# Retention chunks rotated by GpSimd during attention, their low parts split in two halves on VectorE

## The chip, the cores and the metric

The kernel runs on one core of a Trainium2 chip. The metric is the device time of one execution in microseconds (us). The engines are TensorE (PE; PEld is its weight load), VectorE (DVE), ScalarE (ACT), GpSimd (POOL) and SyncE (SP), which issues most transfers.

## What is computed

One decoder layer over 1024 tokens of width 1024: a projection of the normed input, a branch of causal attention (8 heads), a branch of chunkwise retention (4 heads), both gated, merged, projected out, added to the input and normed. The change concerns the retention branch, which in the reference reads:

```python
q = rotary(q.reshape(B, S, H, RET_QK), positions)
k = rotary(k.reshape(B, S, H, RET_QK), positions) * (RET_QK ** -0.5)
def step(R, chunk):
    qc, kc, vc = chunk
    inner = jnp.einsum('bhqk,bhkd->bhqd', jnp.einsum('bhqd,bhkd->bhqk', qc, kc) * decay_in[None], vc)
    cross = jnp.einsum('bhqd,bhde->bhqe', qc, R) * xi[None, :, :, None]
    R = R * gamma_c[None, :, None, None] + jnp.einsum('bhkd,bhke->bhde', kc * zeta[None, :, :, None], vc)
    return R, inner + cross
mu = jnp.mean(out, axis=-1, keepdims=True)
var = jnp.mean(jnp.square(out - mu), axis=-1, keepdims=True)
out = ((out - mu) * lax.rsqrt(var + EPS)).reshape(B, S, RET_WIDTH) * g_ret
```

## The kernel before

Every float32 product is made of three matmuls on rounded operands (fp32r): high times high, high times low, low times high. ScalarE makes the high part of a tile (a Copy), VectorE the low part (tile minus high part), so each operand costs both an instruction. All engines run a program written out by hand and meet at semaphores; each is strictly in order, and so is SyncE's list of transfers.

**Attention** (about 750 to 1080 us) has 64 steps g: head h = g // 8, block of 128 queries i = g % 8. TensorE makes the scores of step g, matmuls of filler work (the retention values v, in units of 24 matmuls that go through `v_stage` to memory), every second step the product with the values of a head, and the transposes of the probabilities of step g - 1. VectorE takes the row maximum (L2021), ScalarE the exponential (L1551), VectorE scales by the reciprocal (L2042, `prob`), and both split the transposed probabilities (L1564, L2052). Every second step VectorE multiplies a pair of outputs by the head's gate (L2033, `y_full`); the gates of two heads are held in two buffers `head_gate`, loaded by `load_head_gate` (L921). ScalarE's queue loads the values of a head, `v_head` (L914). SyncE loads q and k of a head (L904 to L908) and stores `y_full` (L940).

**Retention** (about 1080 to 1340 us) has 32 steps n: head n // 8, chunk n % 8. TensorE: `outputs(n)`, `state(n)` (not in the last chunk of a head), filler (rest of the v work in the first steps, then the merge product of the attention branch, L2504), `turn_keys(n + 1)`, `inner_scores(n + 1)`, filler, `turn_outputs(n)` (L2660), filler. VectorE in step n (`vector_retention`, L2124): a few merge units, bn_stats of the outputs (L2137), bn_aggr (L2140), then it waits for ScalarE's square root (L1620), reciprocal (L2142) and two small instructions, the low part of the state (L2153), `low_chunk(n + 1)`, the gated output `y_ret` (L2163), the low part of q and k of chunk n + 2 (`low_qk`, L1598), and in some steps the low part of a merge weight (L616) or of an attention output tile (`y_lo`, L2183). ScalarE makes the root, the high part of the state, the normed output `out_n` (L1630), which `turn_outputs` waits for, and the high parts (`high_qk`, L1594).

The rotation of q and k is GpSimd's: `rotate_chunk` (L1262) runs four instructions per chunk on a raw chunk of 128x512 and its cosine and sine (L1277, L1279, L1281, L1282), in place, in one of three buffers `qk_raw`. Chunks 0 and 1 are rotated at the end of attention, the other 30 within retention. GpSimd also makes the token sums of each pair of outputs (`token_sums`, L1224: four instructions of 128x256, L1231 to L1238). SyncE's `load_qk_chunk` loads raw chunk and tables three or four steps ahead.

Of the kernel before, what the change touches and what calls it, by code (L numbers as in the profile page):

```python
# [14 lines left out]
F32 = mybir.dt.float32  # L15
F32R = mybir.dt.float32r
# [96 lines left out]
PAIR_CHUNKS = NT // 2  # L113
GROUPS_SPLIT = ((0, 1), (2,), (3,), ())
# [34 lines left out]
class Layer:  # L149
# [3 lines left out]
    def __init__(self, nc, sem, a, t, d, out, pools):  # L153
# [66 lines left out]
        self.head_gate = z("head_gate", 40, [P, 2, S])  # L220
# [5 lines left out]
        self.qk_raw = [z("qk_raw_%d" % n, kb, [P, 6, P]) for n, kb in enumerate((56, 59, 4))]  # L226
        self.qk = z("qk_chunk", 62, [P, 2, 8, P], F32R)
        self.by_sine = [z("qk_by_sine_early", 98, [P, 4, P]), z("qk_by_sine", 0, [P, 4, P])]
        self.v_chunk = [z("v_chunk_%d" % n, kb, [P, 2, RET_V], F32R) for n, kb in enumerate((52, 40, 48))]
# [83 lines left out]
    def semaphores(self, sem):  # L313
# [14 lines left out]
        self.x_late = sem("x_t_late_ready")  # L328
# [31 lines left out]
        self.roped = sem("k_pe_roped")  # L360
# [36 lines left out]
        self.gc_loaded = [sem("gate_chunk_loaded_%d" % n) for n in range(3)]  # L397
        self.qk_step = sem("qk_rotation_step")
# [19 lines left out]
        self.t_sums_done = sem("token_sums_done")  # L418
# [20 lines left out]
        self.out_hi_ready = sem("out_w_hi_ready")  # L439
# [343 lines left out]
    def sync(self, sp):  # L783
# [93 lines left out]
        self.load_head_gate(sp, 1)  # L877
# [40 lines left out]
    def load_head_gate(self, sp, h):  # L918
        if h >= 2:
            sp.wait_ge(self.y_done, 4 * (h - 1))  # L920
        sp.dma_start(self.head_gate[:, h % 2, :], self.d["act_t"][h]).then_inc(self.head_gate_loaded[h % 2], 16)  # L921

    def sync_attention(self, sp):
        d = self.d
        parts = 0
        for g in range(STEPS + 4):
# [3 lines left out]
            if i == 5 and 1 <= h < H_MLA - 1:  # L930
                self.load_head_gate(sp, h + 1)
# [4 lines left out]
            if g >= 4 and g % 2 == 0:  # L936
# [4 lines left out]
                    .then_inc(self.y_stored[pair % 2], 16)  # L941
            if g == STEPS - 6:
# [16 lines left out]
            if g == STEPS + 2:  # L959
                self.load_qk_chunk(sp, 2)  # L960
                self.load_qk_chunk(sp, 3)
                self.load_set0(sp, 1)

    def load_qk_chunk(self, sp, n):
        if n >= 3:
            sp.wait_ge(self.k_turned, n - 2)
            sp.wait_ge(self.qk_lo_ready, n - 2)
        h, m = divmod(n, NT)
        sp.dma_start(self.qk_raw[n % 3][:, 0:4, :].rearrange("p c n -> p (c n)"), self.d["qk"][h, m])\
            .then_inc(self.chunk_loaded[n % 3], 16)  # L970
# [1941 lines left out]
```

## Time and profile before

| | us |
|---|---|
| Median of 3 runs | 1586.63 (1585.99 to 1589.74) |
| Profiled execution, its own time | 1586.35 |
| Its span in the profile | 1584.5 |
| TensorE busy | 1540.6 (97%) |
| VectorE busy | 994.8 (63%) |
| ScalarE busy | 667.4 (42%) |
| GpSimd busy | 415.9 (26%) |

The span is what the profile shows of the execution, 1.85 us less than its time. A busy TensorE is one with a matmul under way; a 128x512 matmul is shown with about 0.39 us though the next one starts 0.23 us after it, so gaps shorter than 0.16 us do not show as idle. Time that is lost shows as idle time or as a granted clock (PEclk) below 1. The shares are means over stages with different limits, so the stages are read apart.

### The profile page before, as it was taken

The page shows a single profiled execution, that of the slowest core. Times are in us where ns is not written, and L with a number is a line of the kernel's source. Part 1 is how long each engine was busy: PE and PEld are TensorE (multiplying, and loading weights), DVE is VectorE, ACT ScalarE, POOL GpSimd, SP SyncE. Part 2 cuts the span into 40 slices and gives each one's busy share as a digit, 9 for nine tenths or more (in the row PEclk, how much of TensorE's full clock was granted, in tenths as well). Part 3 has the DMA queues.
Part 4 walks back from the last instruction along what each step waited for, and adds up shares of the span by engine and source line. Part 5 has one row for each costly group of instructions (what it writes and reads, how often), then busy time and mean ns, then how long its engine had stood idle before and what let it go on. Part 6 is the DMA issues. An engine that isn't in the chain of part 4 may idle for free. (4 is left out here: it accounts for less than half of the span.)

```text
span 1584.5 us, 20414 instructions
## 1 busy us (share of the span) xinstructions
PE 1540.6 (97%) x7472; PEld 1287.2 (81%) x7472; DVE 994.8 (63%) x1629; ACT 667.4 (42%) x1144; POOL 415.9 (26%) x350
## 2 busy tenths in 40 slices
PE   5999999999999999999999999999899999999998
PEld 4788888888888888788888888887677888878886
DVE  6884444444444458752666665667988877799644
ACT  7553455543333353342343343434544444445311
POOL 0032233222322200200000000017778783522000
PEclk9999999999999999999999999999999999999999
DMA  9333232333323334699365554546988787889432
GB/s 381 104 136 113 107 113 107 114 108 118 120 106 107 94 108 156 260 413 339 134 207 176 173 200 172 186 140 229 307 268 265 255 271 240 297 286 309 156 107 80
DMA packets 154499, 299.55 MB, mean 189 GB/s; under 512 B 12048, under 2 KB 93072, under 8 KB 145696
## 3 DMA queue, kind: packets, MB, share of 16 engines
q1 hardware_dynamic: 137680, 265.80, 48.5%
q10 hardware_dynamic: 12080, 15.60, 2.9%
q0 software_dynamic: 4640, 16.84, 2.7%
q8 instruction: 60, 0.98, 0.3%
q14 instruction: 39, 0.32, 0.1%
HBM read 196.23 MB, written 100.93 MB: 188 GB/s over the span
## 5 line engine op out<-in xcount | busy, mean ns | idle before, releaser
L1894 DVE TENSOR_TENSOR w_form<-w_pair,w_form 128x512 fp32r<-128x512 f32 x150 | 116.3, 776 | 124.9 <-ACT w_form L1469 123.2
L1469 ACT ACTIVATE w_form<-w_pair 128x512 fp32r<-128x512 f32 x150 | 94.7, 632 | 216.8 <-PE p_banks L2433 211.7
L1551 ACT ACTIVATE prob<-p_banks,neg_max 128x128 f32<-128x128 f32 (+3 forms) x64 | 47.4, 741 | 183.1 <-DVE neg_max L2021 183.1
L1286 POOL DMA_DIRECT2D v_ret<-v_stage x32 | 17.5, 548 | 399.8 <-DVE v_stage L1998 399.5
L2430 PE MATMUL p_banks<-h_hi,w_form 128*128 128x512 f32 x300 | 116.7, 389 | 0.0
L2432 PE MATMUL p_banks<-h_lo,w_form 128*128 128x512 f32 x300 | 116.7, 389 | 0.0
L2433 PE MATMUL p_banks<-h_hi,w_form 128*128 128x512 f32 x300 | 116.7, 389 | 0.0
L1196 POOL TENSOR_TENSOR w_pair<-w_pair 128x512 f32<-128x512 f32 x25 | 32.5, 1299 | 235.4 <-DVE w_form L1894 235.4
L2712 PE MATMUL p_banks<-t_hi,w_hi 128*128 128x512 f32 x224 | 87.5, 390 | 2.2 <-DVE t_lo L1662 2.2
L2715 PE MATMUL p_banks<-t_hi,w_lo 128*128 128x512 f32 x224 | 87.2, 389 | 0.0
L2714 PE MATMUL p_banks<-t_lo,w_hi 128*128 128x512 f32 x224 | 87.2, 389 | 0.0
L616 DVE TENSOR_TENSOR w_lo<-w_raw,w_hi 128x1024 fp32r<-128x1024 f32 (+3 forms) x63 | 66.8, 1063 | 27.7 <-ACT w_hi L595 27.0
L2472 PE MATMUL p_banks<-w_hi,h_hi 128*128 128x512 f32 x192 | 78.5, 409 | 0.6 <-DVE w_lo L616 0.6
L2430 PE MATMUL p_banks<-h_sum_hi,w_form 128*128 128x512 f32 x200 | 77.8, 389 | 0.0
L2432 PE MATMUL p_banks<-h_sum_lo,w_form 128*128 128x512 f32 x200 | 77.8, 389 | 0.0
L2433 PE MATMUL p_banks<-h_sum_hi,w_form 128*128 128x512 f32 x200 | 77.8, 389 | 0.0
L2430 PE MATMUL p_banks<-h_forms,w_form 128*128 128x512 f32 x200 | 77.8, 389 | 0.0
L2432 PE MATMUL p_banks<-h_forms,w_form 128*128 128x512 f32 x200 | 77.8, 389 | 0.0
L2433 PE MATMUL p_banks<-h_forms,w_form 128*128 128x512 f32 x200 | 77.8, 389 | 0.0
L595 ACT ACTIVATE w_hi<-w_raw 128x1024 fp32r<-128x1024 f32 (+3 forms) x63 | 53.1, 847 | 57.8 <-PE p_banks L2347 13.0
L2472 PE MATMUL p_banks<-w_lo,h_hi 128*128 128x512 f32 x192 | 76.4, 398 | 0.0
L2472 PE MATMUL p_banks<-w_hi,h_lo 128*128 128x512 f32 x192 | 76.2, 397 | 0.0
(348 smaller groups left out, 4482.7 us busy)
## 6 DMA issues: line engine op xcount, KB each, us to landing
w_pair<-in_w_pairs SPq DMA_DIRECT2D x25, 1024.0 KB, 4.8
v_ret<-v_stage POOLq DMA_DIRECT2D x32, 512.0 KB, 3.7
v_chunk<-v_ret SPq DMA_DIRECT2D x32, 512.0 KB, 3.9
w_raw<-in_w_ret SPq DMA_DIRECT2D x28, 512.0 KB, 5.5
w_raw<-in_w_dense SPq DMA_DIRECT2D x23, 512.0 KB, 5.8
act_t<-stage SPq DMA_DIRECT2D x40, 256.0 KB, 2.0
act_t<-stage_late SPq DMA_DIRECT2D x40, 256.0 KB, 2.0
ada<-in_w_ada SPq DMA_DIRECT2D x4, 2048.0 KB, 24.9
```

The costliest lines, as they stand in the source:

```text
L595: self.nc.scalar.activation(self.hi_place(r), self.split_source(r), ACT.Copy).then_inc(self.w_hi_ready, 1)
L616: self.nc.vector.tensor_tensor(self.lo_place(r), self.split_source(r), self.hi_place(r).bitcast(F32), ALU.subtract)\
L1469: self.nc.scalar.activation(self.form[f % FORM_SLOTS][:, 0, :], self.form_source(f), ACT.Copy).then_inc(self.form_hi, 1)
L1551: nc.scalar.activation(self.prob[:, g % 2, 0:width], p[:, 6:8, :].rearrange("p a n -> p (a n)")[:, 0:width], ACT.Exp, bias=self.neg_max[:, ...
L1894: nc.vector.tensor_tensor(self.form[f % FORM_SLOTS][:, 1, :], self.form_source(f), self.form[f % FORM_SLOTS][:, 0, :].bitcast(F32), ALU.su ...
L2430: self.nc.tensor.matmul(out, w_hi[:, cut], x_hi[:, q, :], start=fresh and q == 0, stop=False, skip_group_check=True)
L2432: self.nc.tensor.matmul(out, w_hi[:, cut], x_lo[:, q, :], start=False, stop=False, skip_group_check=True)
L2433: last = self.nc.tensor.matmul(out, w_lo[:, cut], x_hi[:, q, :], start=False, stop=q == KD // 2 - 1, skip_group_check=True)
L2472: ins = self.nc.tensor.matmul(self.p[:, FILL_BANKS[unit % 3], :], h[:, k, tok], w[:, cut], start=(k == 0 and kind == 0), stop=(k == KD - 1 ...
L2712: self.nc.tensor.matmul(out, self.w_hi[:, slot, cut], x_hi, start=fresh and k == 0, stop=False, skip_group_check=True)
L2714: self.nc.tensor.matmul(out, self.w_hi[:, slot, cut], x_lo, start=False, stop=False, skip_group_check=True)
L2715: done = self.nc.tensor.matmul(out, self.w_lo[:, slot, cut], x_hi, start=False, stop=k == KD - 1, skip_group_check=True)
```

## The change

The rotation moves out of retention. In attention, every second step, SyncE (`move_rotation`) stores the chunk that was rotated before to `d["qk"]` and loads the next one with its tables into a place of its own (`rot_raw`, `rot_table`); GpSimd rotates it into `by_sine`. In retention the loaded chunk is the rotated one, with no tables (128 KB fewer per chunk), and TensorE and ScalarE wait for its load instead of GpSimd. To make room, `head_gate` has one buffer instead of two: the gate of head h + 1 is loaded when the last `y_full` of head h is done. `v_chunk` 1 and 2 change places, and their first loads move. `low_qk` becomes two instructions of 128x256: the second half of chunk n + 1 stands behind bn_aggr of step n, ahead of the reciprocal; the first half of chunk n + 2 where the whole was. Some semaphores are shared, with counts that go on from an earlier use. The diff, without the semaphores' names:

```diff
@@ load_head_gate (one buffer)
-        if h >= 2:
-            sp.wait_ge(self.y_done, 4 * (h - 1))
-        sp.dma_start(self.head_gate[:, h % 2, :], self.d["act_t"][h]).then_inc(self.head_gate_loaded[h % 2], 16)
+        if h:
+            sp.wait_ge(self.y_done, 4 * h)
+        sp.dma_start(self.head_gate[:, :], self.d["act_t"][h]).then_inc(self.head_gate_loaded[h % 2], 16)
@@ sync_attention
-            if i == 5 and 1 <= h < H_MLA - 1:
-                self.load_head_gate(sp, h + 1)
...
+                if q == NT // 2 - 1 and head < H_MLA - 1:
+                    self.load_head_gate(sp, head + 1)
+            if g >= 2 and g % 2 == 0:
+                self.move_rotation(sp, g // 2 - 1)
...
-            if g == STEPS - 1:
-                sp.wait_ge(self.y_done, 4 * (H_MLA - 1))
-                self.load_v_chunk(sp, 1)
             if g == STEPS + 1:
                 sp.wait_ge(self.score_done, STEPS)
-                self.load_v_chunk(sp, 2)
+                self.load_v_chunk(sp, 1)
...
+                sp.wait_ge(self.y_done, 4 * H_MLA)
+                self.load_v_chunk(sp, 2)
                 self.load_set0(sp, 1)
+
+    def move_rotation(self, sp, n):
+        if n:
+            h, m = divmod(n - 1, NT)
+            sp.wait_ge(self.qk_step, 4 * n)
+            sp.dma_start(self.d["qk"][h, m], self.by_sine[:, :, :].rearrange("p c n -> p (c n)")).then_inc(self.rot_stored, 16)
+        if n < CHUNK_STEPS:
...
+            sp.dma_start(self.rot_raw[:, :, :].rearrange("p c n -> p (c n)"), self.d["qk"][h, m]).then_inc(self.rot_loaded, 16)
+            sp.dma_start(self.rot_table[:, :, :], self.d["ret_tables"].rearrange("a p n -> p a n")[:, :, m * P:(m + 1) * P])\
+                .then_inc(self.rot_loaded, 16)
@@ gpsimd
-            if g == STEPS - 2:
-                for n in range(2):
-                    self.rotate_chunk(pool, n)
-        for n in range(2, CHUNK_STEPS):
-            if n == 9:
+            if g % 2 and 1 <= g // 2 <= CHUNK_STEPS:
+                self.rotate_chunk(pool, g // 2 - 1)
+        for k in range(1, CHUNK_STEPS, 2):
+            self.token_sums(pool, k)
+            if k == 3:
                 for unit in range(units, FILL_UNITS):
                     self.store_fill(pool, unit)
-            self.rotate_chunk(pool, n)
-            if n >= 4 and n % 2 == 0:
-                self.token_sums(pool, n - 3)
-        for k in (CHUNK_STEPS - 3, CHUNK_STEPS - 1):
-            self.token_sums(pool, k)
@@ low_qk
-    def low_qk(self, dve, n):
+    def low_qk(self, dve, n, half):
         dve.wait_ge(self.qk_hi_ready, n + 1)
-        self.nc.vector.tensor_tensor(self.qk[:, n % 2, 4:8, :], self.qk_raw[n % 3][:, 0:4, :],
-                                     self.qk[:, n % 2, 0:4, :].bitcast(F32), ALU.subtract).then_inc(self.qk_lo_ready, 1)
+        blocks = slice(2 * half, 2 * half + 2)
+        self.nc.vector.tensor_tensor(self.qk[:, n % 2, 4 + 2 * half:6 + 2 * half, :], self.qk_raw[n % 3][:, blocks, :],
+                                     self.qk[:, n % 2, blocks, :].bitcast(F32), ALU.subtract).then_inc(self.qk_lo_ready, 1)
@@ vector_retention
             nc.vector.bn_aggr(self.mean_var[:, s, :], self.stats[:, s, :]).then_inc(self.stats_done, 1)
+            if n + 1 < CHUNK_STEPS:
+                self.low_qk(dve, n + 1, 1)
             dve.wait_ge(self.rooted, 6 + n + 1)
...
             if n + 2 < CHUNK_STEPS:
-                self.low_qk(dve, n + 2)
+                self.low_qk(dve, n + 2, 0)
```

On VectorE, in a retention step behind the outputs' statistics, there stood (`mean_var` is what bn_aggr makes, `ret_rstd` the reciprocal root):

```order
L2140 BN_AGGR mean_var<-stats 128x2
L2142 RECIPROCAL ret_rstd<-ret_root 128x1
L2145 TENSOR_SCALAR ret_rstd<-ret_rstd,ret_cols 128x1
L2148 TENSOR_SCALAR ret_shift<-mean_var,ret_rstd 128x1
L2153 TENSOR_TENSOR state_lo<-p_banks,state_hi 128x512 x2
```

and now:

```order
L2150 BN_AGGR mean_var<-stats 128x2
L1605 TENSOR_TENSOR qk_chunk<-qk_raw_122,qk_chunk 128x256
L2154 RECIPROCAL ret_rstd<-ret_root 128x1
L2157 TENSOR_SCALAR ret_rstd<-ret_rstd,ret_cols 128x1
L2160 TENSOR_SCALAR ret_shift<-mean_var,ret_rstd 128x1
```

A half of a chunk's low parts now stands ahead of the reciprocal. At the end of step 4 of retention there stood on VectorE:

```order
L2121 TENSOR_TENSOR inner_lo<-p_banks,inner_hi 128x128
L2163 TENSOR_TENSOR y_ret_stage_135<-p_banks,gate_chunk 128x512
L1598 TENSOR_TENSOR qk_chunk<-qk_raw_120,qk_chunk 128x512
L2183 TENSOR_TENSOR y_lo_168<-y_raw_169,y_hi_167 128x1024
L2183 TENSOR_TENSOR y_lo_171<-y_raw_172,y_hi_170 128x1024
```

and now:

```order
L2131 TENSOR_TENSOR inner_lo<-p_banks,inner_hi 128x128
L2175 TENSOR_TENSOR y_ret_stage_136<-p_banks,gate_chunk 128x512
L1605 TENSOR_TENSOR qk_chunk<-qk_raw_120,qk_chunk 128x256
L2195 TENSOR_TENSOR y_lo_169<-y_raw_170,y_hi_168 128x1024
L2195 TENSOR_TENSOR y_lo_172<-y_raw_173,y_hi_171 128x1024
```

Here 128x512 became 128x256; the rest is as it was. On SyncE, where one attention head hands over to the next (`q_odd`, `k_odd` are the operands of the head after it), there stood:

```order
L940 DMA y_mla<-y_full 128x256 x2
L904 DMA q_odd<-q_hl 128x2048
L905 DMA k_odd<-k_hl 128x2048
L908 DMA q_rope_odd<-qr_hl 32x1024 x4
L940 DMA y_mla<-y_full 128x256
L921 DMA head_gate<-act_t 128x1024
```

and now:

```order
L940 DMA y_mla<-y_full 128x256
L923 DMA head_gate<-act_t 128x1024
L971 DMA qk_chunks<-qk_by_sine 128x512
L979 DMA rotation_raw<-qk_chunks 128x512
L980 DMA rotation_table<-ret_tables 128x2x128
L906 DMA q_odd<-q_hl 128x2048
L907 DMA k_odd<-k_hl 128x2048
L910 DMA q_rope_odd<-qr_hl 32x1024 x4
```

The gate's load moved ahead of q and k, from one `y_full` later, and the store and two loads of a rotation stand between them.

## Rows read from the trace of the kernel before

**Rows 1.** Stretches of the program: busy time of each engine, clock, DMA.
```profile
core 0: us, PE busy (x) PEld busy (x) DVE busy (x) ACT busy (x) POOL busy (x), PEclk, DMA share, GB/s
760.00:1080.00 320.00, 319.79 (x1851) 278.20 (x1850) 205.06 (x436) 120.37 (x262) 23.88 (x36) 1.00 0.49 169
1084.30:1119.20 34.90, 32.45 (x153) 26.20 (x152) 29.34 (x67) 18.14 (x35) 26.73 (x26) 0.95 0.79 264
1119.20:1156.20 37.00, 30.02 (x137) 22.35 (x137) 34.15 (x69) 18.03 (x33) 29.19 (x27) 0.95 0.93 319
1156.20:1216.00 59.80, 57.70 (x293) 47.49 (x291) 49.31 (x127) 27.21 (x57) 48.21 (x48) 1.00 0.80 255
1216.00:1314.00 98.00, 97.80 (x494) 81.37 (x493) 79.50 (x205) 44.31 (x93) 78.58 (x79) 1.00 0.80 257
```

**Rows 2.** Who TensorE waited for, 1084 to 1330 us (total, times, longest).
```profile
PE p_banks L2660 <- ACT out_n L1630: 8.8, 8, 2.5
```

**Rows 3.** Timeline of all engines, end of retention step 4 and start of 5.
```profile
1125.09 4.54 DVE L2183 TENSOR_TENSOR y_lo<-y_raw,y_hi 128x1024 fp32r<-128x1024 f32 x2
...
1126.40 2.15 POOL L1279 TENSOR_TENSOR qk_raw<-qk_raw 128x512 f32<-128x512 f32 x1
...
1129.56 0.68 DVE L2137 BATCH_NORM_STATS2 stats<-p_banks 128x6 f32<-128x512 f32 x1
...
1131.74 0.78 ACT L1630 ACTIVATE out_n<-p_banks,ret_shift,ret_rstd 128x512 f32<-128x512 f32 x1
...
1132.57 0.66 PE L2660 MATMUL p_banks<-ident,out_n 128*128 128x128 f32 x4 [2.49 <-ACT out_n L1630]
```

**Rows 4.** VectorE's groups by form, 1119.4 to 1156.1 us.
```profile
L2183 DVE TENSOR_TENSOR y_lo<-y_raw,y_hi 128x1024 fp32r<-128x1024 f32 x5 | 9.7, 1966 | 0.0
...
L1598 DVE TENSOR_TENSOR qk_chunk<-qk_raw,qk_chunk 128x512 fp32r<-128x512 f32 x4 | 3.6, 904 | 0.0
L616 DVE TENSOR_TENSOR w_lo<-w_raw,w_hi 128x1024 fp32r<-128x1024 f32 x2 | 3.5, 1754 | 0.0
...
L2118 DVE TENSOR_TENSOR k_tok<-p_banks,k_tok 128x256 fp32r<-128x256 f32 x4 | 1.7, 417 | 0.4 <-ACT k_tok L1606 0.4
```

**Rows 5.** VectorE's groups by form in attention, 760 to 1060 us.
```profile
L616 DVE TENSOR_TENSOR w_lo<-v_weight_raw_odd,w_hi 128x1024 fp32r<-128x1024 f32 x6 | 7.3, 1224 | 0.6 <-ACT w_hi L595 0.3
...
L2042 DVE TENSOR_SCALAR prob<-prob,recip 128x1024 f32<-128x1024 f32 x7 | 5.3, 754 | 0.2
```

**Rows 6.** GpSimd's groups by form, 1084 to 1314 us.
```profile
L1279 POOL TENSOR_TENSOR qk_raw<-qk_raw 128x512 f32<-128x512 f32 x30 | 41.6, 1386 | 2.4
...
L1237 POOL TENSOR_TENSOR y_ret_stage<-y_ret_stage,y_ret_stage 128x256 f32<-128x256 f32 x14 | 11.2, 800 | 1.1
```

**Rows 7.** Who VectorE waited for, 1084 to 1330 us.
```profile
DVE ret_rstd L2142 <- ACT ret_root L1620: 14.1, 31, 0.5
```

**Rows 8.** Timeline in attention where one head hands over to the next.
```profile
838.31 0.53 ACTq L914 DMA_DIRECT2D v_head<-v_hl  x1
...
841.38 0.41 DVE L2033 TENSOR_TENSOR y_full<-p_banks,head_gate 128x256 f32<-128x256 f32 x1
...
842.18 0.43 SPq L904 DMA_DIRECT2D q_odd<-q_hl  x1
...
842.40 0.42 DVE L2042 TENSOR_SCALAR prob<-prob,recip 128x384 f32<-128x384 f32 x1
...
845.40 0.28 PE L2558 MATMUL p_banks<-pt_hi,v_head 128*128 128x256 f32 x1
...
846.04 0.51 PE L2580 MATMUL p_banks<-ident,prob 128*128 128x128 f32 x3
...
850.79 0.41 DVE L2033 TENSOR_TENSOR y_full<-p_banks,head_gate 128x256 f32<-128x256 f32 x1
```

**Rows 9.** DMA issues: KB each, median us from issue to landing.
```profile
v_head<-v_hl ACTq DMA_DIRECT2D x7, 1024.0 KB, 5.9
...
head_gate<-act_t SPq DMA_DIRECT2D x8, 512.0 KB, 6.7
```

More of the change, by code:

```diff
@@ L961, in sync_attention @@
                 self.load_qk_chunk(sp, 3)
+                sp.wait_ge(self.y_done, 4 * H_MLA)
+                self.load_v_chunk(sp, 2)
                 self.load_set0(sp, 1)
+    def move_rotation(self, sp, n):
[4 more added lines that the diff above has]
+        if n < CHUNK_STEPS:
+            h, m = divmod(n, NT)
+            if n == 0:
+                for slot in range(4):
+                    sp.wait_ge(self.stored[slot], 16 * PAIRS)
+            elif m == 0 and h == H_RET // 2:
+                sp.wait_ge(self.raw_stored, 16 * RAW)
+            sp.dma_start(self.rot_raw[:, :, :].rearrange("p c n -> p (c n)"), self.d["qk"][h, m]).then_inc(self.rot_loaded, 16)
+            sp.dma_start(self.rot_table[:, :, :], self.d["ret_tables"].rearrange("a p n -> p a n")[:, :, m * P:(m + 1) * P])\
+                .then_inc(self.rot_loaded, 16)
     def load_qk_chunk(self, sp, n):
@@ L1226, in token_sums @@
         nc = self.nc
-        before = 4 * (k // 2)
+        before = SUMS_FROM + 4 * (k // 2)
         even, odd = self.y_ret[(k - 1) % 4], self.y_ret[k % 4]
@@ L1262, in rotate_chunk @@
     def rotate_chunk(self, pool, n):
-        raw, late = self.qk_raw[n % 3], int(n >= 12)
-        by_sine = self.by_sine[late]
-        cos, sin = (raw[:, c:c + 1, :].broadcast_to([P, 4, P]) for c in (4, 5))
-        pool.wait_ge(self.chunk_loaded[n % 3], 32 * (n // 3 + 1))
+        raw, by_sine = self.rot_raw, self.by_sine
+        cos, sin = (self.rot_table[:, c:c + 1, :].broadcast_to([P, 4, P]) for c in range(2))
+        pool.wait_ge(self.rot_loaded, 32 * (n + 1))
         if n == 0:
             pool.wait_ge(self.v_stored[2], 16)
-        elif n == 12:
-            for slot in range(3):
-                pool.wait_ge(self.v_stored[slot], 16 * sum(self.v_slot(unit) == slot for unit in range(FILL_UNITS)))
-        if n:
-            pool.wait_ge(self.qk_step, 4 * n)
-        if n >= 3:
-            pool.wait_ge(self.out_done, n - 2)
-        self.nc.gpsimd.tensor_tensor(by_sine[:, :, :], raw[:, 0:4, :], sin, ALU.mult).then_inc(self.qk_step, 1)
-        pool.wait_ge(self.qk_step, 4 * n + 1)
-        self.nc.gpsimd.tensor_tensor(raw[:, 0:4, :], raw[:, 0:4, :], cos, ALU.mult).then_inc(self.qk_step, 1)
+        else:
+            pool.wait_ge(self.rot_stored, 16 * n)
+        self.nc.gpsimd.tensor_tensor(by_sine[:, :, :], raw[:, :, :], sin, ALU.mult).then_inc(self.qk_step, 1)
+        self.nc.gpsimd.tensor_tensor(raw[:, :, :], raw[:, :, :], cos, ALU.mult).then_inc(self.qk_step, 1)
         pool.wait_ge(self.qk_step, 4 * n + 2)
-        self.nc.gpsimd.tensor_tensor(raw[:, 0:2, :], raw[:, 0:2, :], by_sine[:, 2:4, :], ALU.subtract).then_inc(self.qk_step, 1)
-        self.nc.gpsimd.tensor_tensor(raw[:, 2:4, :], raw[:, 2:4, :], by_sine[:, 0:2, :], ALU.add).then_inc(self.qk_step, 1)
+        self.nc.gpsimd.tensor_tensor(by_sine[:, 2:4, :], raw[:, 0:2, :], by_sine[:, 2:4, :], ALU.subtract).then_inc(self.qk_step, 1)
+        self.nc.gpsimd.tensor_tensor(by_sine[:, 0:2, :], raw[:, 2:4, :], by_sine[:, 0:2, :], ALU.add).then_inc(self.qk_step, 1)
     def store_fill(self, queue, unit):
@@ L1627, in scalar_retention @@
             act.wait_ge(self.stats_done, 5 * n + 5)
-            if n >= 2:
+            if n == 0:
+                act.wait_ge(self.qk_step, 4 * CHUNK_STEPS)
+            elif n >= 2:
                 act.wait_ge(self.out_turned, n - 1)
@@ L2059, in vector_attention @@
             if g == STEPS - 1:
-                self.low_qk(dve, 0)
+                self.low_qk(dve, 0, 0)
+                self.low_qk(dve, 0, 1)
             if g == STEPS + 1:
                 self.low_chunk(dve, 0)
-                self.low_qk(dve, 1)
+                self.low_qk(dve, 1, 0)
     def merge_unit(self, dve, unit):
```

43 lines of the change are left out of this document (22 added, 21 removed).

## The prediction, made before the changed kernel was run

> **What bounds the kernel now.** I read the stretches first, then who TensorE waits for, then the timeline at one such wait. In attention TensorE is busy for 319.79 of 320 us with the full clock, VectorE for 205 and GpSimd for 24 [rows 1]: TensorE's own work bounds this stage, and both other engines have room. From retention step 9 on it is the same: 97.80 of 98 us between 1216 and 1314 [rows 1], though GpSimd is busy for 78.6 of them. What is lost lies in steps 0 to 8 and at one head's end. TensorE is idle for 2.45 us in 1084.3 to 1119.2, for 6.98 us in 1119.2 to 1156.2 (steps 4 to 7) and for 2.1 us in 1156.2 to 1216. In the first two of these stretches the granted clock is 0.95 on average, which is 5% of 34.9 and of 37, another 1.75 and 1.85 us. That is 15.1 us in all, and nearly the whole of what any change to retention's other engines can win.
>
> Who ends these waits: TensorE's transposes of the outputs wait 8.8 us in 8 places for the normed output [rows 2]. One of them is in the timeline [rows 3]: two low parts of attention outputs, `y_lo`, take 4.54 us on VectorE, up to 1129.6; only then does VectorE begin the statistics of step 5; ScalarE's normed output starts 2.2 us later, and TensorE, 2.49 us idle, starts at 1132.57. So the cause is VectorE, which comes late to bn_stats. In steps 4 to 7 it is busy for 34.15 of 37 us [rows 1], and of the rest 4 times 0.45 us (14.1 us over 31) is the wait for the square root [rows 7]. It is the bound of these four steps.
>
> It is late partly through GpSimd. A tensor_tensor of 128x1024 with both inputs in SBUF takes 1224 ns in attention [rows 5], but `y_lo` takes 1966 and a weight's low part 1754 ns in steps 4 to 7 [rows 4], and the rotation instruction under the first `y_lo` takes 2.15 us [rows 3] where its mean is 1386 ns [rows 6]. Each holds up the other.
>
> **The change, part by part.**
>
> *Steps 4 to 7* (VectorE bound, so each us less of VectorE is one less of time, until TensorE's idle 6.98 and clock 1.85 us are used up):
> - five `y_lo` from 1966 to 1224 ns: 3.7 us; two weights from 1754 to 1224 ns: 1.1 us.
> - four `low_qk` of 904 ns are 3.6 us now. A half is an instruction of 128x256; the like one in these steps takes 417 ns [rows 4]. The first halves, 4 times 0.42, remain in line, 1.7 us. The second halves fall into the root wait of 0.45 us and cost nothing; without this cover they would cost another 1.7. Gain 1.9 us.
> - given back: GpSimd still makes the token sums, four instructions of 0.8 us [rows 6] for two steps, some 3.2 of 15 us or 21%, where it is busy for 29.2 of 37 us or 79% now. In proportion, 1.3 of the 4.8 us on `y_lo` and weights stays.
>
> Together -5.4 us. Bounds: nothing of it (0, VectorE's place taken by another wait) and all that TensorE loses here (-8.8).
>
> *Steps 0 to 3:* the loss of 4.2 us comes from the same things, with two `y_lo`, and chunks 2 and 3 that GpSimd rotates only after attention, so that their low parts are late. I take -3.8; bounds 0 and -4.2.
>
> *Step 8 and the head ends:* TensorE's 2.1 us [rows 1] follow a late bn_stats too. In the last step of a head there is no state product behind which the statistics could hide, so I take -1.7; bounds 0 and -2.1. From 1216 on only 0.2 us is to be had.
>
> *Waits exchanged.* `turn_keys` and `high_qk` wait for a load instead of for GpSimd. SyncE issues it four steps ahead, and it is 128 KB smaller: nothing. `inner_scores(n)` now also waits for the second half, which stands behind bn_aggr of step n - 1. With TensorE's state product, filler and key transposes between, it hides; at a head's end, where the state product is missing, it may show by some 0.3 us, but there TensorE waits for the normed output right after anyway, so nothing is added.
>
> *Attention, GpSimd.* 30 rotations come to 30 times (2 times 1.39 plus 2 times 0.8) = 131 us, which GpSimd has free (24 of 320 busy). What they may hold up on VectorE: `prob` (once a step, 0.75 us at the widest [rows 5]) and 12 weight parts; the other inputs come from PSUM. One hold-up is at most one rotation instruction, 1.39 us. In the step shown `prob` ends at 842.82 and the transposes start at 846.04, 3.2 us later [rows 8], and VectorE is idle for 115 of 320 us. So nearly all hides. Bounds 0 and, should one hold-up in each head come through whole, 8 times 1.39 = 11 us; I take +0.5, near the lower end, since the room shown is more than twice a hold-up.
>
> The trace shows `prob` of 1024 columns in 754 ns, faster than the 1224 ns of an instruction with two SBUF inputs. The Trainium skill (SBUF — State Buffer, Who interferes with whom) says that a tensor_scalar in such a faster mode and a GpSimd instruction shut each other out of a shared pair of ports for a whole instruction. That speaks against this change; the hold-up counted above is such a one, and rows 3 agree for two SBUF inputs, while no row here shows it for `prob`.
>
> *Attention, transfers.* 32 stores and loads of 256 KB each are added and the tables' 128 KB come here from retention: 0.64 MB per pair of steps of 10 us, 64 GB/s on top of 169 [rows 1]. In SyncE's order, past which these are put, q and k of the next head now stand behind a gate and a rotation; they are for the head after that one, whose scores are several steps away. Nothing, but see the rivals.
>
> Sum: -5.4 - 3.8 - 1.7 - 0.1 + 0.5 = -10.5 us. The profiled execution took 1586.35 us, 0.3 less than the median of the runs: 1575.9, or 1576.2 as a median.
>
> **Rivals.**
>
> *Token sums collide more than in proportion.* They start when `y_ret` of an odd step is done, just where VectorE goes on to `low_qk`, `y_lo` and weights. For it: this order in the code. Against: two of the four wait for a store first. If all of the 4.8 us stayed and half of steps 0 to 3: -10.5 + 3.5 + 1.9 = -5.1, 1581.5 us.
>
> *All of TensorE's loss goes,* since VectorE gets ahead and the clock stays up: -15.1 + 0.5, 1572 us. Against it: in steps 4 to 7 VectorE needs 37 - 5.4 = 31.6 us where TensorE's own work is 37 - 8.8 = 28.2.
>
> *The values of a head come late (slower).* `v_head`, 1 MB, is issued at 838.31 and first used at 845.40, 7.1 us later [rows 8]; it lands after 5.9 [rows 9]. That leaves 1.2 us, seven times. In the change a gate (0.5 MB), a rotation's store and loads (0.64 MB) are issued in these 7 us. At 319 GB/s, the rate of a busy stretch [rows 1], they are 3.6 us. If all went ahead of the values, these would land 2.4 us too late, seven times, 16.7 us with TensorE at a stand: -10.5 + 16.7 = +6.2, 1592.8 us. It decides from a landing of 7.1 us on. Against it: at 842.18 the kernel before issues q of the next head, 1 MB, in the very place of the gate [rows 8], and the values are in time all the same.
> The single gate buffer is alike: from one `y_full` to the next are 9.4 us [rows 8], a gate lands after 6.7 [rows 9] at worse places in the queue than its new one.
>
> *It doesn't bind where I think:* ScalarE or TensorE themselves hold up the normed output, and only the contention in steps 0 to 3 goes: about -3, 1583.5 us. Against it is the timeline [rows 3].
>
> **The numbers.** Forecast (-8 to -14) 0.57; token sums collide or a part only (-5 to -8) 0.13; all goes (below -14) 0.08; it binds elsewhere (-1.5 to -5) 0.08; the transfers eat it up 0.14, of which half ends within 0.3% and half slower. A measurement of this kernel can tell about 0.3%, 4.8 us, from no change. Faster by more: 0.57 + 0.13 + 0.08 = 0.78; within: 0.08 + 0.07 = 0.15; slower 0.07. The range from 1570 (all but the last of the loss goes) to 1583 us (a third of the forecast) leaves out the transfers and little else.
>
> **What would show it.** Right: in retention `y_lo` and weights at 1.2 to 1.4 us, halves at 0.42 us, the wait for the root gone from VectorE's list; TensorE's waits for the normed output at 2 to 4 us instead of 8.8; steps 4 to 7 some 5 us shorter with TensorE's clock at 0.97 or more; attention as long as before within 1 us. Wrong: `v_head` or the gate in the list of waits at each head's start; attention longer by several us; `y_lo` still at 1.7 us or more.

## The result and the profile after: nothing won, 5 us lost

| | before | after |
|---|---|---|
| Median, both on the same chip, 8 runs each | 1586.43 us | 1591.55 us (1588.46 to 1593.02) |
| Ratio, 95% interval | | 1.0029 [1.0019, 1.0039] |
| Span of the profiled execution | 1584.5 us | 1588.5 us |

The forecast was 1576.2 us. Here and below a time is the median of several executions, while stage lengths and waits come from one profiled execution of each kernel, and executions of one kernel differ by 5 us and more. To see where the forecast gain went, the span is cut at marks that every kernel has: VectorE's first `prob` of attention, and bn_stats of retention steps 0, 4, 8 and 16 and of step 31, as the traces stamp their starts:

| us | attention | steps 0-3 | 4-7 | 8-15 | 16-30 |
|---|---|---|---|---|---|
| before | 329.94 | 34.95 | 36.95 | 59.78 | 114.30 |
| after | 333.10 | 41.43 | 31.87 | 58.98 | 114.27 |
| difference | +3.16 | +6.48 | -5.08 | -0.80 | -0.03 |

These add up to +3.7 of the 4.0 us by which the span grew. Steps 4 to 7 did as forecast. The stretches of the kernel after, cut at the same marks (attention as in [rows 1]):

```profile
760.00:1080.00 320.00, 316.89 (x1828) 274.99 (x1827) 212.34 (x433) 119.68 (x262) 141.19 (x146) 1.00 0.66 222
1087.00:1128.40 41.40, 32.78 (x152) 26.39 (x151) 27.34 (x72) 18.18 (x35) 9.45 (x12) 0.92 0.91 307
1128.40:1160.20 31.80, 29.64 (x138) 21.57 (x138) 29.75 (x72) 18.06 (x33) 7.10 (x10) 1.00 0.98 353
1160.20:1219.20 59.00, 58.21 (x292) 47.58 (x291) 47.23 (x134) 27.48 (x57) 12.58 (x16) 1.00 0.73 237
```

TensorE has its full clock in steps 4 to 7 (0.95 in [rows 1]) and is idle for 2.2 us instead of 7. In attention it is idle for 3.1 us where it was for 0.2; in steps 0 to 3 for 8.6 of 41.4, at a clock of 0.92. VectorE's groups in steps 4 to 7, against [rows 4]:

```profile
L2195 DVE TENSOR_TENSOR y_lo<-y_raw,y_hi 128x1024 fp32r<-128x1024 f32 x6 | 7.2, 1220 | 0.2 <-ACT y_hi L1661 0.2
L1605 DVE TENSOR_TENSOR qk_chunk<-qk_raw,qk_chunk 128x256 fp32r<-128x256 f32 x8 | 3.6, 444 | 0.0
L619 DVE TENSOR_TENSOR w_lo<-w_raw,w_hi 128x1024 fp32r<-128x1024 f32 x2 | 3.0, 1512 | 0.3 <-ACT w_hi L598 0.3
```

`y_lo` is back at 1220 ns, the halves take 444. Who waited from 1080 to 1330 us (total, times, longest), against [rows 2]:

```profile
ACT out_n L1639 <- POOL qk_by_sine L1288: 8.2, 1, 8.2
PE p_banks L2672 <- ACT out_n L1639: 7.3, 1, 7.3
PE p_banks L2627 <- DVE qk_chunk L1605: 2.3, 5, 0.9
```

All eight waits for the normed output of the kernel before (in steps 1 and 4 to 8 and two later ones, none in step 0) are gone, and a new one of 7.3 us stands in step 0. ScalarE's `out_n` waited there for GpSimd's last rotation. The timeline at it:

```profile
1087.66 0.32 SPq L971 DMA_DIRECT2D qk_chunks<-qk_by_sine  x1
1088.03 0.43 SPq L979 DMA_DIRECT2D rotation_raw<-qk_chunks  x1
1089.01 1.28 SPq L1004 DMA_DIRECT2D v_chunk<-v_ret  x1
...
1093.38 1.25 POOL L1284 TENSOR_TENSOR qk_by_sine<-rotation_raw,rotation_table 128x512 f32<-128x512 f32 x1 [5.22 <-DMA rotation_table<-ret_tables]
1096.61 0.72 POOL L1288 TENSOR_TENSOR qk_by_sine<-rotation_raw,qk_by_sine 128x256 f32<-128x256 f32 x1
1097.43 0.78 ACT L1639 ACTIVATE out_n<-p_banks,ret_shift,ret_rstd 128x512 f32<-128x512 f32 x1 [8.18 <-POOL qk_by_sine L1288]
1097.72 0.93 SPq L989 DMA_DIRECT2D qk_raw<-qk_chunks  x2
1098.26 1.11 PE L2672 MATMUL p_banks<-ident,out_n 128*128 128x128 f32 x4 [7.26 <-ACT out_n L1639]
```

The rotation is a loop in series: SyncE waits for a rotation, stores it and loads the next (1087.66 to 1088.5), the tables land 5 us later, GpSimd takes 4 us, and SyncE can go on at 1097.36. `out_n` lies at the place of `rot_raw`, and a wait in the change's ScalarE part keeps it off (`if n == 0: act.wait_ge(self.qk_step, 4 * CHUNK_STEPS)`). Behind this wait TensorE's clock falls, to 0.50 from 1096 to 1100 us and 0.65 from 1100 to 1104. SyncE's list stands behind the same loop: retention's chunks 2 and 3 are issued at 1097.72, and for the whole execution:

```profile
SPq L971 <- POOL qk_by_sine L1288: 170.5, 29, 9.9
POOL qk_by_sine L1284 <- DMA rotation_table<-ret_tables: 165.2, 30, 11.5
```

In attention one wait of TensorE shows, and what VectorE waited for then was the gate: `y_full` comes at 1014.32 us after a wait of 2.7, `v_stage` right after it, TensorE at 1015.46 (760 to 1080 us):

```profile
PE p_banks L2484 <- DVE v_stage L2007: 3.0, 1, 3.0
DVE y_full L2042 <- DMA head_gate<-act_t: 4.3, 2, 2.7
```

VectorE's scaling of the probabilities has grown from 754 ns [rows 5], by its groups in attention:

```profile
L2051 DVE TENSOR_SCALAR prob<-prob,recip 128x1024 f32<-128x1024 f32 x8 | 8.7, 1092 | 0.3
```

`v_head` was not late. The theory from here: **(a)** retention's gain is real and as large as forecast; **(b)** its start is lost to the last turns of the rotation, through `out_n`'s place and through SyncE's list; **(c)** attention pays for the rotation, by its transfers, by GpSimd beside VectorE, or both. The rival: the halves, or a smaller gain than thought.

### The profile page after: what moved, and what is told of

Read it like the earlier page. It is cut to its first block, busy times and chain, and to the rows that moved or that the text cites. A ratio compares the mean times of both kernels' runs of the same rounds, so it can differ in the third digit from the quotient of the medians.

```text
span 1588.5 us, 20511 instructions
## 1 busy us (share of the span) xinstructions
PE 1541.7 (97%) x7472; PEld 1286.7 (81%) x7472; DVE 995.3 (63%) x1661; ACT 668.1 (42%) x1144; POOL 401.5 (25%) x350
## 4 chain that ended last, share of the span: by engine, by line
PE 63%; DMA 14%; POOL 9%; DVE 7%; issue 3%; ACT 2%; SPq 2%; ACTq 0%; POOLq 0%; DVEq 0%
PE p_banks L2444 10%; PE p_banks L2445 10%; PE p_banks L2442 10%; DMA rotation_table<-ret_tables 9%; PE p_banks L2516 5%; PE p_banks L2484 3%; POOL rotation_raw L1285 2%; PE p_banks L2357 2%; PE p_banks L2358 2%; PE p_banks L2359 2%; POOL qk_by_sine L1284 2%; PE p_banks L2755 2%; PE p_banks L2753 2%; PE p_banks L2754 2%; POOL qk_by_sine L1287 1%
## 5 line engine op out<-in xcount | busy, mean ns | idle before, releaser
L1284 POOL TENSOR_TENSOR qk_by_sine<-rotation_raw,rotation_table 128x512 f32<-128x512 f32 x32 | 42.1, 1315 | 165.3 <-DMA rotation_table<-ret_tables 165.2
```

What stands on the lines that cost most here:

```text
L1284: self.nc.gpsimd.tensor_tensor(by_sine[:, :, :], raw[:, :, :], sin, ALU.mult).then_inc(self.qk_step, 1)
```

## Experiments

**Is the gain there without the rotation?** This kernel leaves the rotation out altogether: no GpSimd instructions, no stores and loads of a turn, no waits for them; the retention works on chunks that aren't rotated.

```diff
-                self.move_rotation(sp, g // 2 - 1)
-                self.rotate_chunk(pool, g // 2 - 1)
-        sp.wait_ge(self.rot_stored, 16 * (n + 1))
-            if n == 0:
-                act.wait_ge(self.qk_step, 4 * CHUNK_STEPS)
```

> Leaves the rotation out of the changed kernel altogether: GpSimd's four instructions per chunk, the loads and stores around them, and the waits on them; the chunks are used unrotated. One head gate and the halves stay. It bounds what the change could win if the rotation cost nothing. Theory A: attention as short as before (retention's step 0 starts at 1084 us), retention 10 to 12 us shorter than before: 1575 to 1578 us. Theory B the same, so this run sets the scale only; above 1580 us the gain in retention is not from GpSimd's and VectorE's relief.

Measured: 1576.95 us, ratio 0.9948 [0.9935, 0.996]. Attention 329.88, then 30.54, 31.88, 59.27 and 114.19 us: against before -4.4, -5.1, -0.5 and -0.1. (a) stands.

**The halves alone**, on the kernel before (`low_qk` in two instructions as in the change, nothing else).

> Kernel before with only the low parts in halves (second half ahead of the reciprocal); rotation in retention as before. Theory: four steps bound by VectorE become 0.4 to 0.5 us shorter each, some other late statistics too, together 2 to 4 us: 1582.5 to 1584.5 us. Rival 1: the half gets in the way of the reciprocal, because GpSimd's rotation holds it up there (up to 1.4 us for one instruction): no gain or slower, 1586 to 1589 us. Rival 2: the halves are what shortened steps 4 to 7 by 5 us in the changed kernel, so all of it is here too: 1579 to 1581 us.

Measured: 1587.28 us, 1.0005 [0.9996, 1.0014]. From 1083 to 1330 us TensorE no longer waits for the normed output, but as long for the halves:

```profile
PE p_banks L2619 <- DVE qk_chunk L1599: 9.0, 6, 2.8
```

As long as VectorE is slowed by GpSimd, the second half ahead of the root only changes which result is late. Steps 4 to 7 take 36.27 us.

**`out_n` in places of its own.**

```diff
-        self.out_n = z("out_n", 44, [P, 2, RET_V])
+        self.out_n = [z("out_n_even", 60, [P, RET_V]), z("out_n_odd", 6, [P, RET_V])]
-            if n == 0:
-                act.wait_ge(self.qk_step, 4 * CHUNK_STEPS)
```

> Changed kernel with the two places of the normed output (out_n) moved off the rotation's input and tables (to 60 and 6 KB), so that step 0's normed output no longer waits for the last rotation. Nothing else moves. Theory A (the rotation loop of load, rotation and store ends at 1097 us, and all that stands behind it comes late): the 7.3 us wait of TensorE for out_n in step 0 is gone, but SyncE still issues v_chunk 1 at about 1089 and chunks 2 and 3 at about 1098, behind the last two rotations, so TensorE waits there instead, 2 to 5 us: 1586 to 1588 us, against 1591.5 for the change. Theory B (the wait is only where lateness from attention, contention and transfers, becomes visible): nothing gained, 1590 to 1592 us. Theory C (this one wait is all): 1580 to 1583 us.

Measured: 1592.19 us, 1.004 [1.0027, 1.0054]: nothing gained. Three of the waits of TensorE, 760 to 1340 us, in the profiled execution, the slowest of six at 1597.9 us:

```profile
PE p_banks L2625 <- DVE qk_chunk L1605: 5.8, 5, 3.6
PE p_banks L2639 <- issue: 5.2, 1, 5.2
PE p_banks L2482 <- DVE v_stage L2005: 2.6, 1, 2.6
```

`outputs(1)` (L2639) waits 5.2 us. The profile names no releaser ("issue"), but by the program it waits for its values, and these are loaded from 1095.56 on, right behind a turn's issues at 1094.21 to 1095.05. The wait had a second one behind it, in SyncE's list.

**The same, and SyncE's first loads of retention ahead of the last turns.**

```diff
-            if g >= 2 and g % 2 == 0:
+            if g >= 2 and g % 2 == 0 and g < STEPS:
                 self.move_rotation(sp, g // 2 - 1)
...
                 self.load_set0(sp, 0)
+                self.move_rotation(sp, CHUNK_STEPS - 1)
...
                 self.load_set0(sp, 1)
+                self.move_rotation(sp, CHUNK_STEPS)
```

> As the run before, and SyncE issues the loads of v_chunk 1, three gates, output tile 0, chunks 2 and 3, v_chunk 2 and output tile 1 ahead of the last two turns of the rotation loop instead of behind them. Theory A: no wait of TensorE over 1 us in steps 0 and 1, granted clock 1.0 there, 1580 to 1583 us, some 9 us below the change. Theory B: 1589 us or more.

Measured: 1585.13 us, 0.9993 [0.9983, 1.0003], some 6 us under the change; steps 0 to 3 in 34.21 us. So (b) is shown: both waits had to go together. (The order alone was not run. But the last rotation ends at 1101.2 us here, and the first `out_n` starts at 1092.21; in its old place it would have waited 9 us.) What is left is 8 us against the kernel without rotation, 3.7 of them in steps 0 to 3 and 4.3 in attention (334.20), where VectorE's `y_full` waits for the gate (DVE, 1000 to 1080 us) and TensorE behind it:

```profile
DVE y_full L2042 <- DMA head_gate<-act_t: 2.8, 1, 2.8
PE p_banks L2484 <- DVE v_stage L2007: 3.1, 1, 3.1
```

**Is the gate late because SyncE issues it late?** The gate's load goes to ScalarE's queue.

```diff
-                if q == NT // 2 - 1 and head < H_MLA - 1:
-                    self.load_head_gate(sp, head + 1)
...
+                if g % NT == 3 and g > NT:
+                    self.load_head_gate(act, g // NT)
```

> e6_place_order (1585.1 us), and the gate of the next head is issued by ScalarE's queue in the third step of the head instead of by SyncE behind a turn of the rotation loop. Theory A (SyncE waits for the rotation with the gate's load behind it, so VectorE waits for the gate, 5.1 us in 2 places, and TensorE for VectorE, 3.1 us): VectorE's wait for the gate is gone, attention 3 us shorter: 1581 to 1583 us. Rival (the gate is late because the transfer engines are full, or contention in attention costs as much elsewhere): 1584 to 1586 us.

Measured: 1585.46 us, 0.9995 [0.998, 1.0011]; TensorE's wait for `v_stage` is still 2.7 us, `y_full`'s for the gate 3.8 in 2. The edit hardly moves the load at the two heads that wait: it is issued 4.8 and 4.2 us after the start of the last `y_full` of the head before, where it was 4.8 and 4.7, so that it says little about a late issue by itself. The kernel without rotation says more. It issues these two loads just as late (4.8 and 4.2 us), and yet VectorE waits 1.0 us at the first and not at all at the second, where `y_full` starts 5.1 us after the issue; in this run it starts 7.1 us after it. So what the rotation adds at these heads is a slower landing, not a later issue. The same kernel with `low_qk` whole again:

> e7_place_order_gate with the low parts whole again at the end of the step. Theory (from e3_split_only, where the halves gained nothing and TensorE waited 9.0 us for the second half): the halves are worth little in either kernel, since they trade the wait for the normed output for one for the second half: within 2 us of e7_place_order_gate. Rival (without rotations beside it the second half fits into the root's wait and saves 0.4 us in each late step): 2 to 4 us slower than e7_place_order_gate, with 3 us or more of waits for out_n.

Measured: 1586.44 us, 0.9995 [0.9983, 1.0008]. Less than a measurement can tell from the halves.

**GpSimd issues the loop's transfers itself**, on the kernel with `out_n` in places of its own.

```diff
-            if g >= 2 and g % 2 == 0:
-                self.move_rotation(sp, g // 2 - 1)
...
+                self.move_rotation(pool, g // 2)
```

> e1_place (1592.2 us), and GpSimd issues the store and the loads of its rotations from its own queue, so that SyncE's list waits for no rotation. Theory A: gate, v_chunk 1 and chunks 2 and 3 are issued on time again though the loop itself is no faster; no wait of TensorE over 1 us from 740 to 1110 us; 1578 to 1582 us, near the kernel without rotation (1577.0). Rival 1: the loop grows, since the three issues cost GpSimd 0.6 us each, and the stores of the retention values behind it come late: TensorE or ScalarE wait for v_stage, 1583 to 1590 us. Rival 2 (lateness is not SyncE's list's): as e1_place, 1590 us or more.

Measured: 1588.22 us, 1.0018 [0.9998, 1.0038]. Retention's start is free (30.28 us for steps 0 to 3), but GpSimd now waits in its own list with v's stores behind it, and attention takes 341.61 us: `y_full` waits 6.2 us for the gate, TensorE 4.3 behind it and 1.4 for `v_head`.

**The gate in two halves**, each loaded when its two pairs are done, so that the one buffer is a ring of two.

```diff
-        sp.dma_start(self.head_gate[:, :], self.d["act_t"][h])
+        h, half = divmod(j, 2)
+        sp.dma_start(self.head_gate[:, 512 * half:512 * half + 512], self.d["act_t"][h][:, 512 * half:512 * half + 512])
```

> Built on the kernel with out_n in places of its own and the retention's first loads ahead of the last two rotation turns (1585.13 us); the head's gate is loaded in two halves of 512 columns, each when its two pairs are done, so that the single 4 KB buffer works as a ring of two. If the 3 us that TensorE waited for v_stage at 1015 us came from the gate with its one buffer (VectorE's y_full waited 5.1 us in 2 for it), that wait and the wait of y_full for head_gate go, and the time is 1582 (1579 to 1584). If the gate was only the first of several transfers that come late in that crowd, another wait of 2 to 3 us stands in its place (v_stage for v_ret, inner_lo) and the time stays at 1585.

Measured: 1583.32 us, 0.9972 [0.9958, 0.9985]. VectorE's list of waits has no `head_gate` any more, attention takes 330.89 us, and the wait at 1015 us is 0.2. The single buffer was the cause, together with the fuller queues: its load can start only when the last `y_full` has read it, and without the rotation's transfers it is still in time for TensorE.

**Rotation by token block**, one load of the tables for four heads' chunks, the chunk used last rotated last:

```diff
-            h, m = divmod(n, NT)
+            m, h = divmod(n, H_RET)
```

> As the kernel with the gate in halves, and the rotation goes by token block, four heads to each, so that one load of rotation_table serves four chunks (24 loads of 128 KB fewer) and the chunk that is rotated last is the one that is used last. If the loop is bound by the sum of its store, loads and rotation, its turn hardly shortens (raw 4.5 us and table 4.7 us run side by side), but the traffic falls by 3 MB in 17; of the about 8 us between the kernel without rotation (1576.95) and the one with places and order (1585.13), traffic theory: a fifth comes back, 1.5 us, with the gate's 2 to 3: 1580 to 1582. If the loss comes from GpSimd's work beside VectorE, nothing beyond the gate's part comes back. Retention's start shows no wait over 1 us on a rotated chunk.

Measured: 1584.14 us, 0.9983 [0.9969, 0.9996]. Steps 0 to 3 take 30.56 us, as without rotation; attention takes 338.61, with waits of TensorE for `v_head` of 1.7 us (until 889) and 2.6 us (until 932). Here the prediction's rival comes true at two heads: the load behind the longer wait landed after 9.7 us.

**What do the transfers cost alone, and GpSimd alone?**

```diff
# transfers alone (GpSimd's call of rotate_chunk is left out)
-            sp.wait_ge(self.qk_step, 4 * n)
+            sp.wait_ge(self.rot_loaded, 32 * n)
...
+            if n:
+                sp.wait_ge(self.rot_stored, 16 * n)
# GpSimd alone (SyncE's move_rotation once, for the first chunk)
-            pool.wait_ge(self.rot_stored, 16 * n)
+            pool.wait_ge(self.y_done, n)
+            pool.wait_ge(self.qk_step, 4 * n)
```

> Transfers of the rotation alone: SyncE loads chunk and table and stores the chunk back unchanged, 32 turns; GpSimd's four instructions of each turn are left out, so that the retention works on chunks that aren't rotated (out_n in places of its own). Against 1576.95 us without any rotation. If the cost inside attention is the transfers' (queues fuller, gate and v parts late), this stands at 1581 to 1585. If it is GpSimd's work, it stands within 1.5 us of 1577.

> GpSimd's part of the rotation alone: its four instructions run 32 times, one turn to each two steps of attention, always on the same chunk, which is loaded once; no transfers of a turn, no waits of the retention on it, chunks not rotated (out_n in places of its own). Against 1576.95 us. If GpSimd's accesses slow VectorE or ScalarE in attention (32 turns of about 4.1 us beside them), 1579 to 1583, and the mean of VectorE's reductions and products in attention grows. If not, 1576 to 1578 and those means stay.

Measured: transfers alone 1580.98 us, 0.9951 [0.9937, 0.9964], attention 333.49; GpSimd alone 1587.09, 1.0001 [0.9988, 1.0013], attention 342.32. In both, steps 0 to 3 take 30.55 us. The transfers' cost is small: 3.6 us more attention in the one execution shown, with waits of TensorE for `v_head` (2.0 us in 2) and for `v_stage` (1.2), but as whole times this kernel and the one without rotation (0.9951 and 0.9948 of before) can't be told apart. SyncE still waits here for each turn's load and store, so it is not the traffic alone. GpSimd's cost is clear: some 9 us of median time over the kernel without rotation, more than all of the change's in attention. The profiled execution of this kernel is the slowest of 12 (1591.89 us), so its 12.4 us in attention are at the upper end. VectorE's groups in attention in the kernel with GpSimd alone:

```profile
L619 DVE TENSOR_TENSOR w_lo<-v_weight_raw_odd,w_hi 128x1024 fp32r<-128x1024 f32 x6 | 16.3, 2712 | 0.3
L2028 DVE TENSOR_REDUCE neg_max<-p_banks 128x1 f32<-128x1024 f32 x8 | 9.8, 1224 | 0.3
```

TensorE's longest wait there:

```profile
PE p_banks L2549 <- ACT prob L1557: 6.3, 3, 2.1
```

and one of the three places in the timeline:

```profile
1028.80 3.79 DVE L619 TENSOR_TENSOR w_lo<-v_weight_raw_odd,w_hi 128x1024 fp32r<-128x1024 f32 x1
1028.95 1.31 POOL L1284 TENSOR_TENSOR qk_by_sine<-rotation_raw,rotation_table 128x512 f32<-128x512 f32 x1
1030.21 1.29 POOL L1285 TENSOR_TENSOR rotation_raw<-rotation_raw,rotation_table 128x512 f32<-128x512 f32 x1
1031.58 1.61 POOL L1287 TENSOR_TENSOR qk_by_sine<-rotation_raw,qk_by_sine 128x256 f32<-128x256 f32 x1
1032.83 1.09 DVE L2028 TENSOR_REDUCE neg_max<-p_banks 128x1 f32<-128x896 f32 x1
...
1035.11 0.80 PE L2549 MATMUL p_banks<-k_even,q_even 128*128 128x512 f32 x1 [2.09 <-ACT prob L1557]
```

`w_lo` (1.22 us alone) all but stands still under two rotation instructions that run at full speed, 1.31 and 1.29 us; the row maximum, which reads PSUM, keeps its 1224 ns (the same without rotation). Behind the 3.79 us the row maximum, the exponential and TensorE come late. Then the clock drops (length, busy PE, PEld, DVE, ACT, POOL, clock, DMA):

```profile
1034.00:1038.00 4.00, 2.89 (x7) 2.33 (x8) 2.20 (x5) 1.82 (x4) 3.53 (x3) 0.62 0.10 33
1038.00:1044.00 6.00, 6.00 (x41) 5.47 (x40) 3.36 (x6) 2.19 (x4) 0.77 (x2) 0.97 0.00 1
```

Three such places are 6.3 us of waits and, at a mean clock of 0.63, 0.57 and 0.62 for 4 us each (0.50, the lower of its two levels, 1.2 GHz, for most of each), some 4.7 us of clock: 11 of the 12.4 us by which attention is longer.

**The same work at another moment.** GpSimd's turn waits until VectorE has done `prob` and, where there is one, `w_lo` of the step.

```diff
+        pool.wait_ge(self.prob_done, g + 1)
+        pool.wait_ge(self.w_lo_ready, R_V + V_PARTS + self.parts_used(g - 1))
```

> GpSimd's part alone as in the kernel at 1587.09 us, with one edit: each turn starts only when VectorE has done its last instruction of the step that has both its tensors in SBUF (prob scaled, and w_lo where the step has one), instead of right at y_full. If the 10 us over 1576.95 come from those two kinds of instruction standing still while GpSimd's run (w_lo 4.06 us instead of 1.23 in the longest, prob 39.6 us in 62 instead of 32.6), and from TensorE's lower granted clock behind each wait for prob, this stands at 1577 (1576 to 1580), w_lo back at 14.7 us in 12. If GpSimd's 4 us of each turn cost wherever they stand, the time stays at 1584 or more.

Measured: 1579.28 us, 0.9957 [0.9945, 0.9969], attention 331.78. `w_lo`:

```profile
L619 DVE TENSOR_TENSOR w_lo<-v_weight_raw_odd,w_hi 128x1024 fp32r<-128x1024 f32 x6 | 7.8, 1293 | 0.1
```

In the profiled executions 10.5 of the 12.4 us in attention are gone, with the same instructions; against before, the medians differ by some 7 us. One part of the expectation missed: `prob` did not go back (39.7 us in 62, as before the edit, 32.7 without rotation), so that slower `prob` costs at most the 1.9 us that attention is still longer; it is `w_lo` that stands in front of a step's chain. Put on the kernels with gate halves and by token block:

> The kernel with the gate in halves (1583.32 us) and the same edit on GpSimd's turns: a turn waits for the step's scaled prob and its w_lo. Its turns start a micro-second later, and the loop of store, loads and rotation has about that much slack in 10 us. If contention with VectorE made part of its loss, the time falls by 1 to 3 us to 1581 (1579 to 1583), and VectorE's prob in attention goes from 42.2 us in 62 towards 33. If the later turns push the loop out of its 10 us, the loads of retention's last chunks come late and the time rises to 1585 or more.

> The kernel that rotates by token block (1584.14 us) with the same edit on GpSimd's turns. Here the chunks rotated last are those used last, so a loop that slips costs retention's start nothing. Contention theory: 1581 to 1582.5; if its loss is only TensorE's wait for v_head (2.6 us in the longest, with the lower granted clock behind it), it stays at 1584.

Measured: 1583.3 us, 0.9979 [0.9968, 0.999], and 1584.99 us, 0.9986 [0.9975, 0.9996]: no gain. In the full kernel the loop through SyncE already keeps the turns mostly off `w_lo` (longest 1.71 us with gate halves), and the added wait keeps them off no better (longest 2.26 us). In the profiled execution, at 1587.25 us the second slowest of 12, later turns also make step 0 longer, 14.0 instead of 10.8 us.

**The last turns behind retention's loads.**

```diff
-                self.move_rotation(sp, CHUNK_STEPS - 1)
             if g == STEPS + 2:
...
                 self.load_set0(sp, 1)
-                self.move_rotation(sp, CHUNK_STEPS)
+                self.move_rotation(sp, CHUNK_STEPS - 1)
@@ sync_retention
+            if n == 1:
+                self.move_rotation(sp, CHUNK_STEPS)
```

> The kernel with the gate in halves (1583.32 us), where steps 0 to 3 of retention still take 34.5 us instead of the 30.5 without rotation: SyncE's loads of chunks 2 and 3 are issued at 1090.5, behind a wait for a rotation. Here SyncE issues these loads first and comes to the last two turns after them (the last store after step 1's output). If those 4 us come from the place in SyncE's list alone, they go: steps 0 to 3 in 30.5 to 31 us and 1579.5 us (1578.5 to 1581). If they come from full transfer queues at that time, the time stays at 1582 to 1584 us.

> The same with GpSimd's turns waiting for the step's scaled prob and w_lo. In the kernel at 1583.30 us this wait gained nothing in time while step 0 grew to 14.0 us (10.8 without it), because the last turns and with them SyncE's loads came later still. With the loads ahead of the last turns that cost is gone: 1578 to 1579.5 us if the wait saves anything in attention, the same as the kernel without it (within 1 us) if it doesn't; 1583 or more if the loop slips in attention too.

Measured: 1580.05 us (1576.91 to 1581.03), 0.9955 [0.9942, 0.9969], and 1580.69 us, 0.9965 [0.9953, 0.9978]. The first one's attention is 330.20 us, its steps 31.56, 32.13, 59.27 and 114.24. Chunks 2 and 3 are issued at 1083.42 instead of 1090.53, and steps 0 to 3 take 2.9 us less than with gate halves alone. So most of the rest at retention's start was SyncE's list again; as whole times the two versions' intervals still overlap. This version is faster than both kernels, by 6 us against before: the change's own idea, with `out_n` elsewhere, the gate in halves and the last turns behind the first loads. The added wait of GpSimd changes nothing that can be told.

## Why the prediction was wrong

- **"Steps 4 to 7 ... Together -5.4 us": right.** -5.08, with `y_lo` at 1220 ns as taken and full clock. Inside it the weights stayed at 1512 ns, and the halves took 444 instead of 417.
- **"Steps 0 to 3: I take -3.8": right only where nothing else enters.** Without the rotation -4.4, in the last version -3.4; in the change +6.5.
- **"Waits exchanged ... SyncE issues it four steps ahead ...: nothing" is the step that failed.** At the start nothing was issued ahead: chunks 2 and 3 went out at 1097.72, 10.8 us into step 0. The step named the waits of TensorE and ScalarE for a load, and left out the one of ScalarE for the last rotation before the first `out_n`, and that a turn of the loop takes 10 us (SyncE's store and loads, 5 us of landing, 4 of GpSimd), as long as the two steps it has, so that the last one, issued at 1088.03, ends 10 us into retention. It also never asked what stands behind SyncE's 170 us of waits for a rotation. TensorE's wait in step 0 was 7.3 us. Removing one of the two waits gave nothing, removing both some 6 us, and a better place for the last turns and the gate in halves another 5.
- **"Step 8 and the head ends ... -1.7": too much.** -0.80, and -0.5 without rotation.
- **"Attention, GpSimd ... +0.5": right for the change by its size, wrong in its bound.** Its upper end took one rotation instruction, 1.39 us, as the largest hold-up. A `w_lo` was held for two, 2.57 us, and the clock behind it added three quarters to what TensorE waited; GpSimd alone then cost about the 11 us that were the upper bound, from three places and not from one in each head. That only +0.3 us is left in the best kernel with all rotations in it comes, as far as the traces show, from where its turns happen to fall, and so the right size is partly luck. The rule cited from the Trainium skill (SBUF — State Buffer, Who interferes with whom), that a tensor_scalar in a fast mode and GpSimd shut each other out, agrees with the change's trace as far as that goes: `prob` of 1024 columns takes 1092 ns instead of 754. It cost nothing there: in the change's attention TensorE never waits for `prob`.
- **"Attention, transfers ... Nothing": wrong.** It was the prediction's second failed step, 3.2 us of attention in the change. The rival named the single gate buffer as "alike" to a late `v_head` and dismissed it on a landing of 6.7 against 9.4 us. It left out that at the two heads where it mattered the load is issued only 4.7 and 4.5 us after the `y_full` that frees the buffer. In the change VectorE waited for it at two heads, and at one of these, behind a stretch with a DMA share of 0.99 (1008 to 1012 us), it cost TensorE 3.0 us; with the gate in halves that is gone. The late `v_head` itself showed in three of the other kernels (1.4, 2.0 and 4.2 us), not in the change.

The sum of terms for retention, -11.0, met -10.1 us without rotation. The forecast missed in what the moved work does where it was moved to.

## What to carry to other kernels

When work is moved into a stage with room, price its loop, not its busy time: 131 us of GpSimd in 320 seemed free, but each turn was a chain of store, load and compute as long as its slot. Look for everything that waits for the last turn, also for what shares memory with it, and for what stands behind it in the issuing engine's list; such waits stand one behind another, and removing one alone shows nothing. What a second engine costs depends on which instruction of the first it meets: here one ahead of a step's chain, not the most frequent one. Where a buffer is halved to make room, let it be refilled in halves.

## What the runs showed of the hardware

- VectorE's `w_lo`, started 0.15 us ahead of two rotation instructions, took 3.79 us while those took 1.31 and 1.29. In another of the three places it started 0.43 us ahead and took 4.06, GpSimd 1.30 and 1.28; in the third GpSimd started first. It was not the one that started first that went on. GpSimd's third instruction, which starts 0.08 us after the second ends, is the one that was slowed, 1.61 us instead of 0.74. The Trainium skill (SBUF — State Buffer, Who interferes with whom) says that issue order decides who blocks; these two places go against it, if the stamps are right to 0.15 and 0.43 us.
- After TensorE's wait of 2.09 us at 1033 the granted clock was 0.62 on average from 1034 to 1038. After the change's wait of 3.0 us, from 1012.45 to 1015.46, it stayed at 1.00. The length of a wait alone does not tell what it costs; what else decides was not tried. The change's two stretches (length, busy PE, clock, DMA share, GB/s):

```profile
1012.00:1016.00 4.00, 0.99 (x4) 1.00 0.61 192
1016.00:1020.00 4.00, 4.00 (x27) 1.00 0.76 281
```

- The mean share of the queues in attention does not tell what the transfers cost: at 0.66 the change's attention was 3.2 us longer than before, at 0.69 the last version's 0.3. What the rows show instead is one load at one head's end: the gate, 0.5 MB, was in use 5.1 us after its issue without the rotation's transfers, and in the change VectorE still waited for it 7.3 us after its issue.
